# Turning attention queries and branch B's keys in 32x32 blocks on VectorE, with GpSimd's transfers carrying the blocks between partition quarters

## The reference

```python
for l in range(DEPTH):
    x = x + 0.5 * _swiglu(_rmsnorm(x, ffn1_norm[l]), ...)
    h = _rmsnorm(x, mix_norm[l])
    a_q, a_kv, i_q, i_k, i_w, b_qkv, c_q, c_kv, c_g, m_g = jnp.split(h @ w_in[l], cuts, axis=-1)
    # A: 4 heads of 64, one key head (rope), keys chosen by an index score (i_q, i_k, i_w), top 64 of 256
    # B: 4 heads, rope on queries and keys, block attention
    # C: 8 heads in 2 groups: raw queries against compressed keys (k_cmp),
    #    rope queries against selected keys (S) and window keys (W)
    g = jax.nn.sigmoid(m_g.reshape(B, T, N_BRANCH, D))
    x = x + (g[:, :, 0] * y_a + g[:, :, 1] * y_b + g[:, :, 2] * y_c) @ w_out[l]
    x = x + 0.5 * _swiglu(_rmsnorm(x, ffn2_norm[l]), ...)
```

## Time and profile before

| | |
|---|---|
| median of three timed runs | 1163.64 us (1163.62 to 1163.77) |
| profiled execution, own time | 1163.91 us |
| its span | 1162.2 us |
| PE / PE weight load / DVE / ACT / POOL busy | 1153.9 / 945.9 / 951.5 / 581.7 / 31.9 us |
| DMA, mean over the span | 182 GB/s |

### The profile page before, as it was taken

One profiled execution on the slowest core, in us unless ns is written; L12 is line 12 of the kernel. 1 busy time (PEld: TensorE's weight loads), 2 busy tenths in 40 slices (PEclk: granted clock), 3 DMA queues, 4 the chain that ended last, 5 costly groups with the idle time before them and its releaser, 6 DMA issues.

```text
span 1162.2 us, 16328 instructions
## 1 busy us (share of the span) xinstructions
PE 1153.9 (99%) x5573; PEld 945.9 (81%) x5573; DVE 951.5 (82%) x1788; ACT 581.7 (50%) x757; POOL 31.9 (3%) x67
## 2 busy tenths in 40 slices
PE   9999999999999999999999999999999999999997
PEld 7888888887778888888888888888877788888886
DVE  6877788899977687778887887878999696888777
ACT  6444345447764464344454444454578635434433
POOL 2000000001000000000000000000010000000000
PEclk9999999999999999999999999999999999999999
DMA  8566554765425555655556556556653335655561
GB/s 285 190 214 216 181 188 163 234 203 163 137 80 182 181 157 204 217 191 185 195 177 202 180 173 215 182 189 191 198 180 110 141 135 184 219 181 169 202 234 38
DMA packets 148996, 211.04 MB, mean 182 GB/s; under 512 B 8160, under 2 KB 109136, under 8 KB 148944
## 3 DMA queue, kind: packets, MB, share of 16 engines
q1 hardware_dynamic: 148256, 209.64, 54.5%
q10 hardware_dynamic: 688, 0.71, 0.2%
HBM read 209.28 MB, written 1.05 MB: 181 GB/s over the span
## 4 chain that ended last, share of the span: by engine, by line
PE 99%; DVE 0%; issue 0%; ACT 0%; POOLq 0%; POOL 0%; DVEq 0%
PE ps L1371 30%; PE ps L1373 30%; PE ps L1372 30%; PE ps L1585 2%; PE ps L1421 1%; PE ps L1641 1%; PE ps L1613 1%; PE ps L1390 1%; PE ps L1546 1%; PE ps L1558 0%; PE ps L1765 0%; PE ps L1672 0%; PE ps L1632 0%; DVE x L1000 0%; PE ps L1573 0%
## 5 line engine op out<-in xcount | busy, mean ns | idle before, releaser
L1114 ACT ACTIVATE whi<-raw 128x2048 fp32r<-128x2048 f32 (+1 forms) x195 | 365.9, 1879 | 253.3 <-PE ps L1373 252.2
L536 DVE TENSOR_TENSOR wlo<-raw,whi 128x2048 fp32r<-128x2048 f32 (+1 forms) x195 | 433.9, 2244 | 65.6 <-ACT whi L1114 45.7
L1371 PE MATMUL ps<-whi,ht_hi 128*128 128x512 f32 (+1 forms) x1192 | 465.6, 391 | 0.2
L1373 PE MATMUL ps<-whi,ht_lo 128*128 128x512 f32 (+1 forms) x1192 | 460.8, 387 | 0.0
L1372 PE MATMUL ps<-wlo,ht_hi 128*128 128x512 f32 (+1 forms) x1192 | 460.3, 386 | 0.0
L1373 PEld LDWEIGHTS ps<-whi,ht_lo 128*128 128x128 f32 x1192 | 223.9, 188 | 45.9
L1371 PEld LDWEIGHTS ps<-whi,ht_hi 128*128 128x128 f32 x1192 | 224.0, 188 | 45.0 <-issue 1.4
L1372 PEld LDWEIGHTS ps<-wlo,ht_hi 128*128 128x128 f32 x1192 | 224.1, 188 | 43.9
L598 DVE STREAM_TRANSPOSE scr<-scr 32x128 f32<-32x128 f32 x688 | 208.3, 303 | 10.3
L1371 PE MATMUL ps<-whi,at_hi 128*128 128x512 f32 x304 | 118.5, 390 | 0.0
L1372 PE MATMUL ps<-wlo,at_hi 128*128 128x512 f32 x304 | 118.3, 389 | 0.0
(11 more groups left out here) (176 smaller groups left out, 757.3 us busy)
## 6 DMA issues: line engine op xcount, KB each, us to landing
raw<-in_ffn_w_down_dram SPq DMA_DIRECT2D x88, 512.0 KB, 4.9
raw<-in_w_in_dram SPq DMA_DIRECT2D x88, 512.0 KB, 4.5
raw<-in_ffn_w_gate_dram SPq DMA_DIRECT2D x85, 512.0 KB, 4.0
raw<-in_ffn_w_up_dram SPq DMA_DIRECT2D x85, 512.0 KB, 5.0
raw<-in_w_out_dram SPq DMA_DIRECT2D x16, 512.0 KB, 4.4
raw<-in_w_branch_c_dram SPq DMA_DIRECT2D x8, 512.0 KB, 4.4
raw<-in_w_branch_b_dram SPq DMA_DIRECT2D x4, 512.0 KB, 3.9
raw<-in_w_branch_a_dram SPq DMA_DIRECT2D x4, 512.0 KB, 4.0
```

Source lines behind the costliest of these rows:

```text
L536: nc.vector.tensor_tensor(wlo[:, n, 0:w], raw[:, n, 0:w], whi[:, n, 0:w].bitcast(F32), ALU.subtract).then_inc(lo_done, 1)
L1114: nc.scalar.activation(whi[:, n, 0:w], raw[:, n, 0:w], ACT.Copy).then_inc(hi_done, 1)
L1371: nc.tensor.matmul(o, xh, wh, start=start, stop=False)
L1373: return nc.tensor.matmul(o, xl, wh, start=False, stop=stop)
```

## The change

All queries (A, I, B, C rotary, C raw) and B's keys, 32 blocks of 128x128 in each layer, are turned without PE. DVE turns them inside the quarter of the partitions where they are (`turn_blocks`: 12 instructions of 128 partitions in each layer), GpSimd issues 16 transfers for each of two groups (`cross`), SBUF to SBUF, each 32 partitions x 4 runs of 128 values, 64 KB. The four blocks of a group lie interleaved in the result (`qk_1`, `qk_2`): neighbouring tokens are four values (16 bytes) apart. Group 0 (A, I and B's queries, B's keys) is turned behind slab 8, group 1 (C's) behind the short slab 11. Five fills (10 blocks) stay on PE: four behind the short slabs, one behind slab 13. The attention scale moves from the copies into `maxima` and the copy of C's scores. The zeroing of `cmpm` moves from DVE to GpSimd, behind group 0's transfers. SP waits for group 0 ahead of slab 15 instead of for the fills ahead of slab 18. In the diff's new code, PE's scores of I (e = 0) wait for group 0 and those of C (e = 1) for group 1.

```diff
-FILLS = [((0, 1), "qs", 0), ((2,), "pair", 0), ((6, 7), "qs", 4),
-         ((14,), "pair", 4), ((15,), "pair", 6), ((10, 11), "qs", 6), ((12, 13), "qs", 8),
-         ((16, 17), "n", 0), ((18, 19), "n", 2)]
-NFILL = len(FILLS) + 2
-T1 = 3
-
-DVE_TURNS = {"I": (3, "q", 2), "K": (8, "k", 2)}
+FILLS = [(0, 0), (1, 2), (None, 0), (None, 1), (2, 4)]
+NFILL = len(FILLS)
+EARLY = 4
+
+
 
 
 
 def by_act(f):
-    return f % 2 == 0 if f < T1 else (f - T1) % 2 == 1
+    return f in (0, 3, 4)
...
-            def turn_blocks(l, name, rows=(0, P)):
-
-                b, kind, b0 = DVE_TURNS[name]
-                into = (q_t if kind == "q" else k_t)[:, b0:b0 + 2, :].rearrange("p b (t c) -> p t b c", t=NT)
+            def turn_blocks(l, n):
+
                 own(l)
-                for a in range(*rows, 32):
-                    for q in range(0, P, 32):
-                        step(nc.vector.transpose(into[q:q + 32, :, :, a:a + 32], rs[a:a + 32, :, b:b + 2, q:q + 32]))
+                for t in range(NT):
+                    raw_q = pr[:, t, C_Q:C_Q + 512].rearrange("p (b c) -> p b c", b=4)
+                    for g, src in enumerate((rs_1[:, t, 0:4], rs_1[:, t, 4:8]) if n == 0 else (rs_2[:, t], raw_q)):
+                        for q0, into in [(0, turned_1)] if n == 0 else [(0, turned_2[0]), (2, turned_2[1])]:
+                            dst = into.rearrange("p q (g t c b) -> p q g t b c", g=2, t=NT, b=4)[:, :, g, t]
+                            step(nc.vector.transpose(dst, src.rearrange("p b (q c) -> p q b c", q=4)[:, q0:q0 + into.shape[1]]),
+                                 ("turn", n))
 
             def cmp_windows(l):
 
-                dve.wait_ge(fill_a, (l + 1) * NACT)
+                dve.wait_ge(fill_a, l * NACT + 2)
+                dve.wait_ge(cmpm_zero, l + 1)
...
-                            step(nc.vector.tensor_tensor_reduce(prob_view(b, t)[:, h, :], score_head(t, h), mk, -1.0,
+                            step(nc.vector.tensor_tensor_reduce(prob_view(b, t)[:, h, :], score_head(t, h), mk, -ATT_SCALE,
...
-                step(nc.vector.memset(cmpm[:, :, :, :], 0.0), ("cmpm zero",))
                 last_width = {S + m: nk * LASTU for m, _, nk in M_LAST}
                 for m in range(2, 14):
                     convert(l, S + m, last_width.get(S + m, SLAB))
 
                     if m in (3, 5, 7):
                         rope(l, m // 2 - 1)
-                    if m == 7:
-                        turn_blocks(l, "K", (0, 64))
-                    if m == 9:
-                        turn_blocks(l, "K", (64, P))
+                    if m == 8:
+                        turn_blocks(l, 0)
                     if m == 10:
                         rope(l, 3)
                     if m == 11:
-                        turn_blocks(l, "I")
+                        turn_blocks(l, 1)
                     if m == 12:
                         rope(l, 4)
-                for f in range(T1):
+                convert(l, S + 14)
+                rope(l, 5)
+                for f in range(EARLY):
                     if not by_act(f):
                         fill_out(l, f)
-                rope(l, 5)
-                convert(l, S + 14)
...
+            def cross(l, n):
+
+                wait_step(pool, l, ("turn", n))
+                for a in range(4):
+                    for q in range(4):
+                        dst = (qk_1, qk_2)[n][32 * q:32 * q + 32, :, :, 32 * a:32 * a + 32, :]
+                        src = turned_blocks(n, q)[32 * a:32 * a + 32].rearrange("p (e c) -> p e c", e=2 * NT)
+                        pool.dma_start(dst.rearrange("p g t c b -> p (g t) (c b)"), src).then_inc(crossed[n], 16)
+
             for l in range(DEPTH):
                 norm(l * 3)
                 norm(l * 3 + 1)
+                cross(l, 0)
+                pool.wait_ge(crossed[0], (l + 1) * 256)
+                nc.gpsimd.memset(cmpm[:, :, :, :], 0.0).then_inc(cmpm_zero, 1)
+                cross(l, 1)
...
+                if e < 2:
+                    pe.wait_ge(crossed[e], (l + 1) * 256)
+                qb, kb, _ = heads_of(pair) if pair != "C" else (0,) * 3
...
-                                               kc_t[:, j // 2, :, :].rearrange("p a c -> p (a c)"), qn_t[:, j, :],
+                                               kc_t[:, j // 2, :, :].rearrange("p a c -> p (a c)"),
+                                               qk_2[:, 1, :, :, j],
...
-                    ins = nc.tensor.matmul(score_head(t, h), q_t[row, qb + h // 2, t * P:(t + 1) * P],
-                                           k_t[row, kb + kstep * (h // 2), 0:nk], start=opens, stop=n >= 6,
+                    ins = nc.tensor.matmul(score_head(t, h), queries(row, qb + h // 2, t),
+                                           keys(row, pair, kb, h // 2, t + 1), start=opens, stop=n >= 6,
...
-                wait_step(pe, l, ("rope", 3))
-                for f in range(T1):
-                    if f == 0:
-                        pe.wait_ge(proj_done, l * 12 + 10)
+                wait_step(pe, l, ("rope", 4))
+                pe.wait_ge(proj_done, l * 12 + 10)
+                for f in range(EARLY):
                     fill(l, f)
                 wide(l, S + 13, 0, 4, (0, 1), 512, 0, KD - 1)
                 pe.wait_ge(proj_done, l * 12 + 12)
                 wait_step(pe, l, ("rope", 5))
-                for f in range(T1, NFILL):
+                for f in range(EARLY, NFILL):
...
-                for m in (13, 14):
-                    load_halves(l, S + m, w_in, 512 * (m - 13), 4, M_G, 512)
-                for q in range(2, 12):
-                    if q == 5:
-
-                        sp.wait_ge(fill_ps, (l + 1) * NFILL)
+                for q in range(12):
+                    if q == 2:
+                        sp.wait_ge(crossed[0], (l + 1) * 256)
                         sp.dma_start(w1[0][1], rows_cols(cmp_w1_k, l, 8 * P, 8, 0, P)).then_inc(w1_in[0], 16)
```

More of the change, by code:

```diff
@@ L273, in build @@
         fill_a = sem("fill_a")
+        crossed = [sem(f"crossed{n}") for n in range(2)]
         v_step = sem("v_step")
         cg_done = sem("cg_done")
+        cmpm_zero = sem("cmpm_zero")
         cmp_ps = sem("cmp_ps")
@@ L460, in fill_bank @@
         def fill_bank(f):
[L461 removed]
+            return 4 + f % 4
         def copy_fill(copy, f):
             bank = fill_bank(f)
[L466 to L468 removed]
+            block, b = FILLS[f]
+            if block is None:
+                v = b
                 for g in range(2):
@@ L474, in copy_fill @@
                 return
-            _, kind, b = FILLS[f]
-            if kind == "pair":
-                for g in range(2):
-                    for half in range(2):
-                        copy(k_t[half * HD:(half + 1) * HD, b + g, :], ps[g * HD:(g + 1) * HD, bank, 0:SEQ], 1.0)
-                return
-            into = qn_t if kind == "n" else k_t if kind == "k" else q_t
-            copy(into[:, b:b + 2, :].rearrange("p b c -> p (b c)"), ps[:, bank, :], ATT_SCALE if kind in ("n", "qs") else 1.0)
+            for g in range(2):
+                for half in range(2):
+                    copy(k_t[half * HD:(half + 1) * HD, b + g, :], ps[g * HD:(g + 1) * HD, bank, 0:SEQ], 1.0)
         def load_x(eng, n):
@@ L660, in rope @@
                 dve.wait_ge(proj_done, l * 12 + 2 * u + 2)
-                for c0, nh, b0, part in ROPE[u]:
+                for c0, nh, place in ROPE[u]:
                     src = pr[:, :, c0:c0 + nh * HD].rearrange("p t (h c) -> p t h c", h=nh)
+                    into, b0 = {"first": rs_1, "second": rs_2, "pair": pairs}[place[0]], place[1]
                     if nh == 1:
-                        dst = rs[:, :, b0:b0 + 1, part * HD:part * HD + HD]
+                        dst = into[:, :, b0:b0 + 1, place[2] * HD:place[2] * HD + HD]
                     else:
-                        dst = rs[:, :, b0:b0 + nh // 2, :].rearrange("p t b (e c) -> p t (b e) c", e=2)
+                        dst = into[:, :, b0:b0 + nh // 2, :].rearrange("p t b (e c) -> p t (b e) c", e=2)
                     tmp = rtmp[:, :, 0:nh, :]
@@ L1280, in mixer @@
                 last_width = {S + m: nk * LASTU for m, _, nk in M_LAST}
-                for m in range(2, 14):
+                for m in range(2, 15):
                     convert(l, S + m, last_width.get(S + m, SLAB))
```

93 lines of the change are left out of this document (47 added, 46 removed).

## The result

Before: 1163.62 us, median of 5 runs (1163.22 to 1163.77). After: **1174.49 us**, median of 5 runs (1174.04 to 1176.07). The ratio is 1.0096, 95% interval 1.0081 to 1.0111. I had said 1158.5 us and 1157.0 to 1165.0: wrong in sign, by 16 us.

A forecast was written before the change was run, and what follows sets the result against it. PE was taken as the bound, busy 1153.9 of 1162.2 us. 1163.91 less 5.26 for blocks leaving PE gave 1158.65; the profiled execution was 0.27 above the median, so about 1158.4, stated as 1158.5, range 1157.0 to 1165.0.

The forecast's parts named there:

- What leaves PE: 22 of 24 turned blocks behind slab 13 go: 2.63 us a layer, 5.26 in two; nothing behind the short slabs.
- What DVE gets: DVE's new turning with strided writes: upper bounds 4.9 and 5.6 us, at most the 10.6 us of before.
- the term that decides: GpSimd's two groups of transfers must land before slab 15's transfers, the windows and C's scores; expected in time.
- d: Time for GpSimd to issue one transfer: taken as 0.4 to 0.9 us, must stay below 1.05.
- the rival that I gave 0.17: Transfers late, PE stands before C's scores in both layers: 1174.5, or 1172.5 us if GpSimd stands during conversions; chance 0.17.
- What PE reads now: PE's score operands 16 bytes apart: taken as zero cost; upper bounds 4.4 us for moving values, 20 us for weights.
- weights too: Rival: strided reads also slow PE's weight loads in the scores, 1.4 us in each of 7 steps: 1178 us; chance 0.04.
- the moving side: Strided moving reads in C's and B's scores doubled: 2.2 us a layer, 4.4 in all, giving 1162.9; chance 0.07.
- the forecast's own range: Case of transfers on time and no stride cost: 1158.5 us, range 1157.3 to 1160; chance 0.66.

The follow-up runs named there:

- e10_weight_distances: Kernel before the change, with the queries (PE's weights) of each pair read at another distance, 4 to 64 bytes, on other data: 1172.84 us, one run.
- e2_queries_contig: Changed kernel with only the queries, PE's weights, read side by side (other data); B's keys and C's raw queries stay 16 bytes apart: 1164.24 us.
- e1_contig: Changed kernel with all of PE's reads of the turned blocks (queries, B's keys, C's raw queries) side by side, on other data: 1160.06 us.

## Why the prediction was wrong

- **What leaves PE: right.** 2.53 us a layer against 2.63; nothing behind the short slabs; the windows ended at 261.0 (forecast 261.6), in time.
- **What DVE gets: right, at its upper end.** 1082 ns for 512 values, 605 ns for 256 (upper bounds 1.23 and 0.70 us); group 0 turned by 232.5, group 1 by 244.9.
- **The transfers, "the term that decides": inside its bounds, and it did not decide.** d = 0.55 us (taken 0.4 to 0.9); the landings were 4.25 us and more than 7 behind the last issue and not 2.1, with 10.6 us to spare. The mechanism of the rival that I gave 0.17, GpSimd standing while VectorE converts, is not in the trace. The Trainium skill (SBUF — State Buffer, SBUF: two separate sides) gives it as a block of GpSimd's descriptor writes while VectorE holds the port pair that they share; no run here shows one.
- **What PE reads now: this is the step that failed.** "A read port at half its rate would still feed them. That is why I take zero." The argument compared the mean rate of a stage (1.0 column a ns) with a rate of the products (2.3). It left out that a load reads its 128 columns in one go, 186 ns, and that PE waits for it. The loads' own row of the kernel before, for the scores of I, stood against it:

```profile
267.31 1.39 PEld L1585 LDWEIGHTS ps<-k_t,q_t 64*128 64x128 f32 x16 [0.20 <-issue]
```

  They fill 1.39 of the stage's 1.58 us. In e10_weight_distances, with the keys as before, the stage grows from 1.58 to 2.45 us, 0.87, while eight loads in each half grow by 8 x 0.136 = 1.09. There was almost no slack to eat. The upper bounds stood in the text (2.2 us a layer for moving, 1.4 a stage for weights), the measured ones are 1.83 (B 1.38 and C 0.45, in e2_queries_contig) and 0.87. So the rival "weights too" named the right mechanism, at a chance of 0.04. That its 1178 lies only 3.5 us off is in part luck: it takes 20 us for weights that double (they grew by 0.73) and leaves out the 4.4 us of the moving side beside them. Both together cost 2 x 7.22 = 14.4 us.
- **What the range held.** It ended at 1165.0 and left out that rival, though its price had no row against it. I had given the Trainium skill's rule of two hits in a line, which this layout breaks, a weight for the moving side only. e1_contig, the change without the distance, came out at 1160.06, inside the forecast's own range (1157.3 to 1160) but for 0.06 us: PE gained 4.90 of the 5.26 us there, so the sum of the other terms was good.
- **The end of the program** (1.2 us) was in no term.

## What to carry to other kernels

A layout that spares one engine work is paid by every reader of the data: price the reader's access, operand by operand, before the transfers. When no row shows an access pattern, its upper bound belongs in the range, and a rate averaged over a stage is no slack for a load that the stage waits for. Here half the interleaving (two values in 16 bytes) kept 1.50 and 2.27 us of the 2.53 a layer and cost 0.03 us a stage to read, at twice the runs and almost the same issue time.

## What the runs showed of the hardware that I had not expected

- PE's weight load of 128 float32 columns: 186 ns at 4 bytes, 192 at 8, 254 at 12, 322 at 16, then 305 to 328 up to 64. Moving reads of float32: a stage of 1.58, 1.63, 2.31, 2.96 us, then 2.96 to 3.02.
- Writing at 16 bytes costs VectorE's turn of 512 values 1082 ns, at 8 bytes 678, at 4 bytes 674.
- GpSimd's issue takes 0.53 to 0.65 us whatever the transfer carries (32 or 64 KB, runs of 128 to 512 bytes), and is hardly slower inside VectorE's conversions (0.56 against 0.55 us). ScalarE's issue of the same transfer took 0.63 us.
- The program ended 1.2 us later after 64 of GpSimd's transfers in runs of 512 bytes and 6.4 us later after 128, though all of them had landed hundreds of microseconds earlier; after 64 in shorter runs only 0.1 us later. GpSimd's closing DRAIN took 5.92, 11.14 and 2.00 us.
